# Scores of the sparse attention: one product per head over 64 rows instead of 128 with zeros, two heads side by side

## What is computed

```python
q = rope_2(q, cos[:, :, None], sin[:, :, None])
ss = jnp.einsum('bghqd,bgqkd->bghqk', qb, ks_g).astype(jnp.float32) * scale
p_s = masked_softmax(ss, mask_s[:, :, None])
sw = jnp.einsum('bghqd,bgkd->bghqk', qb, kw).astype(jnp.float32) * scale
p_w = masked_softmax(sw, mask_w)
```

## Time and profile before

| what | us |
|---|---|
| median of 3 runs | 1712.76 (1712.62 to 1718.04) |
| profiled execution | 1711.61 |
| its span on the core | 1709.8 |
| PE busy | 1553.8 (91% of the span) |
| DVE busy | 1138.0 (67%) |
| ACT busy | 880.8 (52%) |
| granted clock of TensorE, mean | 0.957 of full speed |

### The profile page before, as it was taken

The page is one execution under the profiler, slowest core; times in us unless marked ns, Lnnn a source line. Parts: engine busy times, 40 slices in busy tenths (PEclk is TensorE's granted clock), DMA queues, the critical chain, the costliest instruction groups (busy, mean ns, idle before and its releaser), DMA issues.

```text
span 1709.8 us, 28283 instructions
## 1 busy us (share of the span) xinstructions
PE 1553.8 (91%) x11797; PEld 1504.3 (88%) x11797; DVE 1138.0 (67%) x1799; ACT 880.8 (52%) x1564; POOL 88.8 (5%) x141
## 2 busy tenths in 40 slices
PE   4989899799979898997999899999999888899997
PEld 3988899799969888997999789999888777899986
DVE  5653659986667535599866669884676534788755
ACT  3455447564445554475644556653564532566443
POOL 9000000003200000000000100000000000000000
PEclk8999999999999999998999889999899999999998
DMA  4632455466636324563665445555324011455541
GB/s 142 189 94 80 124 173 162 123 185 178 199 89 184 92 83 122 173 172 113 184 203 185 133 131 175 183 174 185 112 89 138 25 50 50 148 179 180 174 159 62
DMA packets 237631, 239.23 MB, mean 140 GB/s; under 512 B 19224, under 2 KB 232274, under 8 KB 237504
## 3 DMA queue, kind: packets, MB, share of 16 engines
q1 hardware_dynamic: 232048, 228.66, 44.0%
q0 software_dynamic: 5456, 8.77, 1.8%
HBM read 236.33 MB, written 1.05 MB: 139 GB/s over the span
## 4 chain that ended last, share of the span: by engine, by line
PE 82%; DVE 7%; ACT 5%; issue 2%; DMA 2%; POOL 1%; DVEq 0%; SPq 0%; POOLq 0%
PE bank L563 24%; PE bank L566 23%; PE bank L567 23%; PE bank L716 2%; PE bank L648 2%; PE bank L1017 1%; DVE rs L1597 1%; ACT w_hi L1122 1%; DVE w_lo L1591 1%; ACT S L1254 1%; PE bank L1003 1%; DMA raw<-in_mla_w_ukv 1%; PE bank L919 1%; DMA raw<-in_w_out 1%; POOL rows L485 1%
## 5 line engine op out<-in xcount | busy, mean ns | idle before, releaser
L563 PE MATMUL bank<-h_hi,w_hi 128*128 128x256 f32 x2344 | 677.4, 289 | 56.7 <-DVE h_lo L1620 23.3
L1591 DVE TENSOR_TENSOR w_lo<-raw,w_hi 128x1024 fp32r<-128x1024 f32 (+1 forms) x460 | 524.6, 1154 | 304.9 <-ACT w_hi L1122 303.5
L566 PE MATMUL bank<-h_lo,w_hi 128*128 128x256 f32 x2344 | 672.6, 287 | 0.0
L567 PE MATMUL bank<-h_hi,w_lo 128*128 128x256 f32 x2344 | 672.2, 287 | 0.0
L1122 ACT CAST w_hi<-raw 128x1024 fp32r<-128x1024 f32 (+1 forms) x460 | 454.1, 990 | 204.4 <-DMA raw<-in_w_in 65.0
L563 PEld LDWEIGHTS bank<-h_hi,w_hi 128*128 128x128 f32 x2344 | 458.3, 196 | 63.4 <-issue 46.3
L566 PEld LDWEIGHTS bank<-h_lo,w_hi 128*128 128x128 f32 x2344 | 458.7, 196 | 0.1
L567 PEld LDWEIGHTS bank<-h_hi,w_lo 128*128 128x128 f32 x2344 | 458.2, 195 | 0.0
L563 PE MATMUL bank<-y_hi,w_hi 128*128 128x256 f32 x352 | 99.7, 283 | 0.0
L567 PE MATMUL bank<-y_hi,w_lo 128*128 128x256 f32 x352 | 99.6, 283 | 0.0
L566 PE MATMUL bank<-y_lo,w_hi 128*128 128x256 f32 x352 | 99.6, 283 | 0.0
(11 more groups left out here) (367 smaller groups left out, 2531.8 us busy)
## 6 DMA issues: line engine op xcount, KB each, us to landing
raw<-in_w_in SPq DMA_DIRECT2D x160, 512.0 KB, 3.8
raw<-in_ffn_up SPq DMA_DIRECT2D x88, 512.0 KB, 3.5
raw<-in_ffn_down SPq DMA_DIRECT2D x32, 512.0 KB, 3.4
raw<-in_w_proj_a SPq DMA_DIRECT2D x16, 512.0 KB, 3.4
raw<-in_w_proj_b SPq DMA_DIRECT2D x16, 512.0 KB, 3.4
raw<-in_w_out SPq DMA_DIRECT2D x16, 512.0 KB, 4.5
raw<-in_ple_gate SPq DMA_DIRECT2D x16, 512.0 KB, 3.4
raw<-in_w_proj_c SPq DMA_DIRECT2D x16, 384.0 KB, 3.2
```

The source lines that it names most:

```text
L563: first = pe.matmul(out_, lh, rh, start=start, stop=False)
L566: pe.matmul(out_, lh, rl, start=False, stop=False)
L567: return pe.matmul(out_, ll, rh, start=False, stop=stop)
L1591: dve.tensor_tensor(w_lo[b][:, 0:size], raw[b][:, 0:size], w_hi[b][:, 0:size].bitcast(F32), ALU.subtract).then_inc(sems["w_split"], 1)
```

## The change

The product of a head takes only the 64 rows in which its queries and keys lie: rows 0 to 63 for head 0, rows 64 to 127 for head 1. The two heads of a tile are issued one behind the other into two banks, their masks after them. S.4 and S.5 now hold one head position each (head n of both tiles) instead of one tile each, so that the two halves of the array write to banks of their own; `maxima`, `exps2` and the waits in `turn2` follow this. `side()` is asked for both banks of a pair ahead of its first product. The zeros in `kz`, and the wait for them, are gone.

```diff
-            pool.wait_ge(sems["x_ready"], KT * (1 + L + 3))
-            pool.memset(kz[:, :, :, :, :], 0.0).then_inc(sems["nsa_zero"], w.given("nsa_zero"))
...
             def scores2(g):
                 pe.wait_ge(sems["q2_ready"], g + 1)
-                for n in range(4):
-                    b = job(f"S{g}.{n}")
-                    pe.matmul(ps[b][:, :], q2[:, 2 * g + n // 2, P:TOK],
-                              kz[:, n % 2, g, :, :].rearrange("p a k -> p (a k)"), start=True, stop=False)
-                    filled(pe.matmul(ps[b][:, :].rearrange("p (a k) -> p a k", a=2)[:, :, P:TOK], ident_r[:, :],
-                                     causal_r[:, :].unsqueeze(1).to_broadcast([P, 2, P]), start=False, stop=True), b)
-                for u in range(2):
-                    b = job(f"S{g}.{4 + u}")
-                    pe.matmul(ps[b][:, :].rearrange("p (a k) -> p a k", a=4), ident_r[:, :],
-                              causal_r[:, :].unsqueeze(1).to_broadcast([P, 4, P]), start=True, stop=False)
-                    for n in range(2):
-                        mm = pe.matmul(ps[b][:, n * TOK:(n + 1) * TOK].rearrange("p (a k) -> p a k", a=2),
-                                       q2[:, 2 * g + u, 0:P], kz[:, n, g, :, 0:P], start=False, stop=n == 1)
-                    filled(mm, b)
+                causal2 = causal_r[:, :].unsqueeze(1)
+                for u in range(3):
+                    names = [f"S{g}.{2 * u + n}" for n in range(2)]
+                    bs_ = [side(n) for n in range(2)]
+                    def masks(n, out_, a, first):
+                        return pe.matmul(out_, ident_r[:, :], causal2.to_broadcast([P, a, P]), start=first, stop=not first)
+                    if u < 2:
+                        for n in range(2):
+                            row = slice(64 * n, 64 * n + 64)
+                            pe.matmul(ps[bs_[n]][:, :], q2[row, 2 * g + u, P:TOK],
+                                      kz[row, n, g, :, :].rearrange("p a k -> p (a k)"), start=True, stop=False)
+                        for n in range(2):
+                            assert job(names[n]) == bs_[n]
+                            filled(masks(n, ps[bs_[n]][:, :].rearrange("p (a k) -> p a k", a=2)[:, :, P:TOK], 2, False), bs_[n])
+                    else:
+                        for n in range(2):
+                            masks(n, ps[bs_[n]][:, :].rearrange("p (a k) -> p a k", a=4), 4, True)
+                        for f in range(2):
+                            for n in range(2):
+                                row = slice(64 * n, 64 * n + 64)
+                                mm = pe.matmul(ps[bs_[n]][:, f * TOK:(f + 1) * TOK].rearrange("p (a k) -> p a k", a=2),
+                                               q2[row, 2 * g + f, 0:P], kz[row, n, g, :, 0:P], start=False, stop=f == 1)
+                                if f == 1:
+                                    assert job(names[n]) == bs_[n]
+                                    filled(mm, bs_[n])
...
-                    emptied(f"S{g}.{4 + u}")
+                    emptied(f"S{g}.4")
+                    emptied(f"S{g}.5")
...
-                            dst, src, e = T0[:, r, 2 * (i - 4) + a // 2, a % 2, :], ps[b][:, a * P:(a + 1) * P], 4 * (i - 4) + a
+                            n = 2 * (a // 2) + i - 4
+                            dst, src, e = T0[:, r, n, a % 2, :], ps[b][:, a * P:(a + 1) * P], 2 * n + a % 2
...
-            dve.wait_ge(sems["nsa_zero"], 2)
+            dve.wait_ge(sems["nsa_zero"], 1)
...
-                        dst, src = nm[:, r, 4 * (i - 4):4 * (i - 4) + 4], ps[b][:, :].rearrange("p (a k) -> p a k", a=4)
+                        dst = nm[:, r, 0:8].rearrange("p (f n a) -> p f n a", f=2, n=2)[:, :, i - 4, :]
+                        src = ps[b][:, :].rearrange("p (f a k) -> p f a k", f=2, a=2)
```

## The result

The changed kernel is slower: 1726.15 us median (1723.12 to 1728.71, 5 runs) against 1712.97, ratio 1.0068, 95% interval 1.0054 to 1.0083. Run again later (e5) it was 1722.57 against 1714.70, ratio 1.0045 (1.0027 to 1.0062). So it costs some 8 to 13 us, 0.5 to 0.7%. The forecast was 1716.4, and the range ended at 1721; both medians lie above it.

What follows compares the result with a forecast made beforehand. TensorE was taken as the bound, though readers of the scores set the pace where the change lies; delays of 2 x 0.67 + 2 x 1.13 = +3.6 us on the 1712.76 median gave 1716.4 us, range 1712 to 1721.

Steps and rivals of the forecast that it cites:

- What bounds the kernel: TensorE, busy 91% of the span, but shorter products pay only where its queue is full; score groups also wait on DVE and ACT.
- The products: In the scores, a pair of 512-column products over 64 rows takes 1.28 us instead of 1.71, by partial overlap.
- 3 of 4: A pair's four product records run in 3 steps, between no overlap (4) and full overlap (2).
- rival B: Both halves overlap fully, a pair costing 0.85 us: +2.3 us, 1715.1, or +0.3 if changing over is free; chance 0.2.
- A0 A1 B0 B1: Program order of the two products' records, by which B0 comes behind A1 and only those two run together.
- The change of shape: Each switch between 64-row products and 128-row masks costs 0.20 us, bounds 0 and 0.48, six times a group.
- The waits: S.4 waits for the banks of S.0 and S.1, 0.90 us longer in groups 0 and 1.
- The direct sum: Delays over the four groups of heads, 0.67 us each in 0 and 1, 1.13 each in 2 and 3: +3.6 us.
- rival C: Stretches of halved TensorE clock come, go or move, 3 us each costing or returning 1.5; two more give +6.6; chance 0.1 upward.
- Slower by over 0.3%: Kernel slower by more than about 5.1 us, from rival A and part of rival C and dearer shape changes; chance 0.25.
- rival A: The two halves of a pair do not overlap at all: +6.6 us, 1719.4; chance 0.2.

Runs made afterwards that it cites:

- e5: The changed kernel run again, unaltered, against the kernel before: 1722.57 us, ratio 1.0045.
- e13: The changed kernel with the extra unread products of e16, more of them in some waits: 1703.42 us, 0.9944 of the kernel before.
- e16: The kernel before with extra unread TensorE products in its five waits and in eleven waits elsewhere: 1693.67 us, 0.9889 of the kernel before.
- e1: The kernel before with one more wait, the first mask of S.4 waiting for the banks of S.0 and S.1: 1720.96 us, ratio 1.0045.
- e15: The changed kernel with both products of a pair in rows 0 to 63, so they cannot overlap: 1732.45 us, 1.0104 of the kernel before.
- e14: The changed kernel's order, banks and waits, but every product over all 128 rows, zeros kept: 1722.37 us, 1.0040 of the kernel before.
- e7: The changed kernel with S.4 and S.5 one behind the other, each waiting for its own bank alone: 1724.70 us, 1.0060 of the kernel before.
- e4: The changed kernel with extra unread products filling five TensorE waits: 1714.46 us, 1.0004 of the kernel before.

## Why the prediction was wrong

**What bounds the kernel.** Right in kind: nothing was won by shorter products, since the scores' readers set the pace, as the earlier trace rows had it. But I took the granted clock as given where the change works, and it is not.

**The products.** The step "3 of 4" failed: all four records pair up, 1.06 us from the first start to the masks, and the change has the full overlap of rival B. The order A0 A1 B0 B1, my argument against it, did not hold the second product back; whether the records were issued in that order no row shows.
By the Trainium skill ("TensorE: Matmul & The Clock Gate", the section on packing small matmuls) tiles in different row groups run concurrently; by that rule the trace agrees, four records in 1.13 us.

**The change of shape.** In group 2 nothing stands between the first pair and the second:

```profile
1365.77 1.13 PE L980 MATMUL bank<-kz,q 64*128 64x512 f32 x4
...
1367.26 1.13 PE L980 MATMUL bank<-kz,q 64*128 64x512 f32 x4
```

Of these 1.49 us 0.85 are the pair's columns and 0.24 the two masks, so 0.40 is left for two changes: the 0.20 that I had taken from the earlier trace rows. Before, two products with their masks took 1.94.

**The waits.** The 0.90 us for the second bank is there (eight ACT instructions in 1.94 us against four in 1.03). The direct sum, 3.6 in the forecast and 2.3 under rival B, was measured at 3.0 (e13 against e16). All of this was right to within a microsecond; that 3.6 is near 3.0 is in part luck, since the overlap was underrated and the delays on the chain were, too.

**The clock, rival C.** Here is the step that failed. I gave it 0.1 and priced it at 3 us, as stretches that "come, go or move", without a direction. It is the larger term: what the direct 3 us leave of the 8 to 13 is 5 to 10. The profiles show 31 us of halved clock in the stage instead of 14, and the mean clock went from 0.956 to 0.948 and 0.951. The size fits: by an estimate from these means, twice 1 less the clock of the time, some 151 us were at the halved clock before and 169 to 180 with the change, and the 18 to 29 more can cost up to half of that, 9 to 14 us (the 24 transposes of e16 lost 1.70 us in a halved stretch of 3.4). The change does two things that both go that way: it lets TensorE stand longer (e1) and it moves products to 64 rows (e15 against e14, and the table behind them). The earlier trace rows stood in my own list; what I left out was to ask what TensorE had been doing before that stretch, and what a change makes of it.

**The chances.** "Slower by over 0.3%" had 0.25 and happened. The range missed because its upper end took rival A's sum and one stretch of clock; a direct cost of 3 us with five or six such stretches (17 us more at the halved clock in the profile) was not among the cases.

What stays open: how the loss divides between the stands and the halves in the changed kernel itself. e1 shows a loss by longer stands without the halves, e15 and e7 one by the halves without longer stands, and the two don't add up to separate shares. The fillers don't divide it either, since they win about as much from the kernel before. Why products over 64 rows are followed by less clock no run shows.

## What to carry to other kernels

Before making TensorE's products shorter in a stage where it waits for others, look at the granted clock there: the time saved becomes standing time, and a longer stand can cost several times its length (e1: 1.8 us direct, 8 in all). Splitting the array in two makes a pair of products as fast as one, with 0.2 us lost at each change to it and from it, but it was worth nothing here and was followed by more halved clock. Where a kernel's profile shows halved stretches after waits of a few us, fill the waits with products that nobody reads, sized by the wait that the timeline shows; here sixteen filled waits gave 1.0 and 1.1%, more than the change took. And judge a change with the same fillers in both kernels: e4 alone looked as if they made up for the change, but the kernel before gained as much.

## What was not expected of the hardware

- The first records of both products of a pair start within one hundredth of a microsecond (the first two of the four records are both at 1321.62 in the timeline, the other two half a microsecond later), although each product is two records and the kernel writes one product behind the other. With both products in one half (e15) the four records took 1.91 us to their masks.
- Products over 64 rows were followed by a granted clock of 0.50 where the same products over 128 rows, in an execution with nearly the same times, kept 1.00 (e15 and e14).
- One execution's halved stretches say little: the runs of the kernel before reach from 1707.08 to 1724.19 us in one series, and the mean of their clocks, 0.956, is what stays from series to series.
